# FoX and dilated attention trunk on one core: the value product in two 64-column halves, issued between the scores and the transposes of a tick

## What is computed

```
for i in range(DEPTH):                       # 2 layers
    h = rmsnorm(x, norm[i])
    x = x + (fox_attention(h) if i % 2 == 0 else dilated_attention(h))
    x = x + square(relu(rmsnorm(x, mlp_norm[i]) @ w1[i])) @ w2[i]

# one head of one group, for a block of queries
s = q @ k.T * scale + bias_or_mask
p = softmax(s)
o = p @ v                                    # the value product
```

## Time and profile before

| | us |
|---|---|
| median of 3 runs | 1651.6 |
| lowest and highest | 1650.48, 1652.94 |
| the profiled execution, its own time | 1654.75 |
| its span from first to last instruction | 1653.0 |
| PE busy | 1611.0 (97%) |
| PE weight loads busy | 1363.1 (82%) |
| DVE busy | 818.0 (49%) |
| ACT busy | 600.4 (36%) |
| POOL busy | 355.3 (21%) |
| mean granted clock of PE | 0.994 |

### The profile page before, as it was taken

How to read it: one execution, slowest core, us unless ns; L and a number is a source line. 1 busy time by engine, 2 the same in 40 slices (tenths; PEclk the granted TensorE clock), 3 DMA queues, 4 the chain that set the end, 5 groups by cost and what they waited for, 6 DMA issues and landing times.

```text
span 1653.0 us, 21763 instructions
## 1 busy us (share of the span) xinstructions
PE 1611.0 (97%) x8058; PEld 1363.1 (82%) x8066; DVE 818.0 (49%) x1468; ACT 600.4 (36%) x1068; POOL 355.3 (21%) x534
## 2 busy tenths in 40 slices
PE   7999988999999999999999999999999999999999
PEld 6777766888888888899998899998777888888887
DVE  4356566444343444444646576546565443435342
ACT  5433332342323233434434443434342432424230
POOL 3412100050000000263527364535711000000000
PEclk9999999999999999999999999999999999999999
DMA  5311110323232323332222412222223232323232
GB/s 169 90 51 39 57 34 3 100 88 104 89 105 85 114 77 104 126 90 77 66 75 77 128 53 77 64 77 64 77 79 103 78 113 87 104 89 102 89 101 78
DMA packets 77556, 139.83 MB, mean 85 GB/s; under 512 B 12192, under 2 KB 12192, under 8 KB 77216
## 3 DMA queue, kind: packets, MB, share of 16 engines
q1 hardware_dynamic: 75280, 134.51, 26.6%
q10 hardware_dynamic: 2192, 4.20, 0.7%
HBM read 132.33 MB, written 6.36 MB: 84 GB/s over the span
## 4 chain that ended last, share of the span: by engine, by line
PE 85%; DVE 5%; POOL 4%; issue 2%; ACT 2%; SPq 1%; DMA 0%; ACTq 0%; POOLq 0%; DVEq 0%
PE ps L467 74%; PE ps L553 3%; PE ps L525 3%; POOL qrs L1330 2%; PE ps L539 2%; PE ps L565 1%; POOL qss L1329 1%; DVE pT_sb L1110 1%; PE ps L498 1%; ACT w_h L784 1%; DVE qss L1021 1%; PE ps L519 1%; ACT p_sb L848 1%; ACT sq L822 1%; DVE negmax L1075 0%
## 5 line engine op out<-in xcount | busy, mean ns | idle before, releaser
L467 PE MATMUL ps<-w_h,act_h 128*128 128x512 f32 x768 | 317.3, 413 | 5.7 <-DVE w_l L995 3.4
L467 PE MATMUL ps<-w_h,act_l 128*128 128x512 f32 x768 | 306.9, 400 | 0.0
L467 PE MATMUL ps<-w_l,act_h 128*128 128x512 f32 x768 | 305.7, 398 | 0.0
L784 ACT ACTIVATE w_h<-w_raw,gain_t 128x512 fp32r<-128x512 f32 x316 | 209.8, 717 | 150.4 <-PE ps L467 102.7
L995 DVE SCALAR_TENSOR_TENSOR w_l<-w_raw,gain_t,w_h 128x512 fp32r<-128x512 f32 x316 | 226.6, 759 | 58.4 <-ACT w_h L784 58.4
L467 PE MATMUL ps<-w_h,hid_h 128*128 128x512 f32 x640 | 252.5, 395 | 0.2
L467 PE MATMUL ps<-w_l,hid_h 128*128 128x512 f32 x640 | 250.0, 391 | 0.0
L467 PE MATMUL ps<-w_h,hid_l 128*128 128x512 f32 x640 | 249.7, 390 | 0.0
L467 PEld LDWEIGHTS ps<-w_h,act_h 128*128 128x128 f32 x768 | 192.2, 250 | 24.0 <-issue 8.0
L467 PEld LDWEIGHTS ps<-w_l,act_h 128*128 128x128 f32 x768 | 192.5, 251 | 15.2
L467 PEld LDWEIGHTS ps<-w_h,act_l 128*128 128x128 f32 x768 | 193.4, 252 | 13.5
(11 more groups left out here) (150 smaller groups left out, 1935.8 us busy)
## 6 DMA issues: line engine op xcount, KB each, us to landing
w_raw<-in_mlp_w SPq DMA_DIRECT2D x128, 512.0 KB, 3.7
w_raw<-in_dil_w_in SPq DMA_DIRECT2D x72, 512.0 KB, 3.7
w_raw<-in_fox_w_in SPq DMA_DIRECT2D x22, 512.0 KB, 3.6
w_raw<-in_fox_w_out SPq DMA_DIRECT2D x8, 512.0 KB, 3.7
w_raw<-in_dil_w_out SPq DMA_DIRECT2D x8, 512.0 KB, 3.8
acc_kept<-acc SPq DMA_DIRECT2D x2, 1056.0 KB, 6.4
o_sb<-acc_kept SPq DMA_DIRECT2D x2, 1056.0 KB, 5.1
x_sb<-in_x SPq DMA_DIRECT2D x4, 512.0 KB, 8.4
```

Source lines behind the costliest of these rows:

```text
L467: return mm(ps_out, lhs[i], rhs[j], start=(k == 0 and term == 0), stop=(k == KT - 1 and term == 2))
L784: last = fn(w_h[:, u % WR, j, :], raw(u)[:, j, :], ACT.Copy, scale=gain_t[:, norm, k:k + 1])
```

## The change

Two edits in the PE program, none elsewhere.

1. Each value matmul of a 128x128 stationary block becomes two, with the block's columns 0 to 63 and 64 to 127 as the stationary operand. The first writes partitions 0 to 63 of the output bank, the second 64 to 127. The moving operand is the same for both. 400 matmuls become 800. In the built program the halves carry the array tile (128 rows, 64 columns) at column 0 and at column 64, where the whole block had (128, 128).
2. Within a tick, `values` (of three ticks ago) is called ahead of `turn_probs` (of two ticks ago), so it stands directly behind the scores where the tick has any.

```diff
--- before.py
+++ after.py
@@ -550,8 +550,10 @@
                 c = 0
                 for q, k0, nk in SCORE_BANKS[SETS[s][0]][i]:
                     for k in range(nk):
-                        last = mm(o_ps[:, q, 0:VC], pT_sb[:, a % 2, c * P:(c + 1) * P], v_sb[s % 2][:, k0 + k, h // 2, head_cols(h)],
-                                  start=(k == 0), stop=(k == nk - 1))
+                        for side in range(2):
+                            rows = slice(side * P // 2, (side + 1) * P // 2)
+                            last = mm(o_ps[rows, q, 0:VC], pT_sb[:, a % 2, c * P + rows.start:c * P + rows.stop],
+                                      v_sb[s % 2][:, k0 + k, h // 2, head_cols(h)], start=(k == 0), stop=(k == nk - 1))
                         c += 1
                 last.then_inc(pv_done, 1)
 
@@ -574,10 +576,10 @@
                             pe.wait_ge(qt_done, QK_SET * (attend + 1))
                         if a < nt and a % 2 == 0:
                             scores(attend, t0 + a)
+                        if 3 <= a <= nt + 2:
+                            values(attend, t0 + a - 3)
                         if 2 <= a <= nt + 1:
                             turn_probs(attend, t0 + a - 2)
-                        if 3 <= a <= nt + 2:
-                            values(attend, t0 + a - 3)
                     for s, b in turns_of_tick(proj, attend, a):
                         turn_qk(s, b)
                     if proj is None:
```

## The result

The changed kernel is slower: 1680.68 us median of 4 runs (1671.05 to 1686.98), before 1652.27 (1650.48 to 1660.79), ratio 1.0137 with a 95% interval of 1.0101 to 1.0172. Forecast were 1653.5 us and a range up to 1668. The changed kernel's runs lie much further apart than those of before, and their order is that of the granted clock: 1671 us at a mean of 0.994, 1677 at 0.991, 1685 at 0.982, 1687 at 0.980. The execution profiled is this last one, 32 us of span above the one before, so it shows more of the loss than the median does (28 us). A straight line through the four times against their mean clocks gives 1666 us at a clock of 1.000; one through the 19 executions of the kernel before that were measured beside the first experiments gives 1648. By this estimate, good to a few us with only four points, about 18 us of the loss are there at full clock, and the rest is the clock.

What follows compares the result with a forecast made beforehand. PE bounds steps with filler, the scores-DVE-exponentials round the other two. Halves -27.5, shape changes +16.8, order +1.8 and +6, steps without filler +4.5 sum to +1.6 us; against a 1651.6 us median, forecast 1653.5, range 1640 to 1668.

Steps and rivals of the forecast that it cites:

- What bounds the kernel: PE time in steps with filler (projection matmuls); in (None,1) and (None,7), the round from scores over DVE to exponentials.
- Part 1, the halves: Value blocks in steps with filler: halves pair up, 0.059 us a pair instead of 0.111, a gain of 27.5 us.
- the rival in which they take turns: Value blocks: the two halves run one after another, so no pairing gain; about 1686 us, chance 0.15.
- Part 2, the change of shape: 72 value blocks in steps with filler: PE loses time switching between whole array and halves, 16.8 us (11 to about 24).
- Part 3, the order with filler: Steps with filler: dearer way from transposes to filler, 1.8 us, and lost cover of waits for DVE's output, 6 us.
- the 3 to 6 named as a sign: PE's idle time at the value line until DVE's output would grow by about 3 to 6 us if right.
- Part 4, the steps without filler: Steps (None,1) and (None,7): later transposes delay DVE, and the clock may lose a little; 4.5 us (0 to 10).
- The claim that the late copy matters in 8 pairs of ticks: Steps (None,1) and (None,7): DVE's copy ends 0.45 us later in 4 + 4 pairs of ticks, 3.6 us.
- part 3b: Steps with filler: transposes no longer run inside the values' wait for DVE's output, at 11 blocks; 6 us (3 to 9).
- a little more: Steps (None,1) and (None,7): with PE idle for longer, the granted clock may cost slightly more, inside the 4.5 us.
- the waits grow: Step (1,0): 15 more value blocks wait 0.5 us each for DVE's output, slower by 4 to 15 us, 1661; chance 0.22.

Runs made afterwards that it cites:

- the first experiments: The follow-up runs starting with the order alone (1709.78 us) and the halves alone (1647.11 us), measured beside the kernel before.
- run 2: Changed kernel with the values back behind the transposes, so the halves alone against the kernel before: 1647.11 us, ratio 0.9958.
- run 6: Kernel before, with 72 added idle-time matmuls in steps (None,1) and (None,7) to keep PE busy: 1654.50 us, ratio 1.0001.
- run 3: Changed kernel with values ahead of the transposes only in steps with filler, old order in (None,1) and (None,7): 1651.37 us, ratio 0.9987.
- runs 4 and 9: Changed kernel with a third probability buffer in steps (None,1) and (None,7), 1661.53 us; the same plus 72 idle-time matmuls there, 1661.22 us.

## Why the prediction was wrong

- **What bounds the kernel**, PE where there is filler and the round over DVE where there isn't: right, and it is where the result was decided.
- **Part 1, the halves**: right. 0.62 us for a block of 16 recorded matmuls against a forecast of 0.616; the rival in which they take turns (0.15) fell, though the measured 1681 us is near its 1686. The rule named beside it, of the Trainium skill, "TensorE: Matmul & The Clock Gate", Part 3, that weight loads overlap running matmuls only where the row group differs, isn't what these rows show: both halves share all rows, and their pairs still start within 0.46 us.
- **Part 2, the change of shape**: right. 0.32 into a value block (0.33), 0.34 out of it into the filler in run 2 (0.34). One sum is written wrongly: from 88.06 + 0.11 to 88.37 it is 0.20; the 0.09 comes out with the second matmul's own slot of 0.11 added.
- **Part 3, the order with filler**: 6.2 us by the run of the order alone, a part of it the clock, and 3.6 to 4.3 with the halves (1041.7 and 1042.4 against 1038.1); 7.8 forecast. PE's idle time at the value line until DVE's output grew by 9.3 us in these steps (4.8 to 14.1), more than the 3 to 6 named as a sign. Parts 1 to 3 together were -2.9 by the sum, and the rest of the stretch came out at -0.5 (1042.4 against 1042.9) in the changed kernel and -1.2 in the run with the new order there only.
- **Part 4, the steps without filler**: wrong, and the step that decided. It said 4.5 us (0 to 10); it was 32.6 in the profiled execution. With every bound of parts 2 to 4 at its high end the sum is +17, some 1669 us, so no other size of its terms reaches the result. Three things failed in it.
  1. The claim that the late copy matters in 8 pairs of ticks, 0.45 each. It was worked out for even ticks alone, from the earlier trace rows. In odd ticks the value block itself waits for DVE's output and the transposes stood ahead of that wait; behind it they hold DVE's copy up by 0.79 us. That was the same loss of cover that part 3b counts where there is filler, and part 4 left it out. Near full clock the late copy and output come to 7.6 us (against run 6) to 10.5 (against run 3) instead of 3.6; the 0.45 itself is by the prediction's own times 236.1 - 235.57 = 0.53.
  2. The exponentials' wait for the transposes (`pt_full`, two buffers) was missing. Part 3b asked who waits behind the value block and named DVE and the filler, and of the exponentials only that the transposes wait for them. The other direction costs 3 to 4 us by itself, and most of the lower clock came by way of it (runs 4 and 9).
  3. The clock was "a little more". It is 20 us of the profiled execution and about 13 of the median. The row was there: a mean of 0.94 with PE busy 44.6 of 55 us says that the lower level is granted at times in this step even before the change. How much more of it the longer rounds would bring, the row doesn't say; the prediction left it some 0.9 us of the 4.5 without working it out.
- The rival *the waits grow* had a part of the mechanism, DVE's outputs that come too late, but its place was the step (1,0), and it was priced without the clock at 1661 us. Its chance was 0.22. The chances gave slower by over 0.2% 0.37 in all, by causes that aren't the one measured.

## What to carry to other kernels

When an instruction is moved ahead of another on an engine, list who waits for the one that is now later, in each stage of the kernel, buffers to be freed included; a wait that was covered in one stage can be the pace of another. Where a stage already shows a granted clock below 1, added waits there can cost more than their length (here 20 us of 32.6), and a run that keeps the engine busy tells the two apart. Try the move stage by stage: here the two parts of the change had opposite signs, and the halves alone (1647 us, ratio 0.9958) beat the kernel before and the changed one.

## What the runs showed of the hardware

- Two 64-column stationary blocks at columns 0 and 64, both of 128 rows and float32, run side by side: eight pairs of recorded matmuls in 0.46 us from first to last start. Their loads are recorded with a mean of 138 ns in run 2, against 192 for 128 columns in the kernel before:

```profile
L555 PEld LDWEIGHTS ps<-v,pT_sb 128*64 128x64 f32 x1600 | 56.8, 138 | 36.9 <-issue 23.0 <-DVE pT_sb L1112 14.0
```

- The gain of pairing is mostly given back by the changes of shape, 0.28 to 0.34 us for each block that stands alone, against an estimate of 8 x 0.052 = 0.42 gained in a block of four. In the steps with filler 4.8 us were left of it (run 2).
- The clock fell to its lower level in stretches where PE was still recorded as busy for most of the time: 70.9 of 91 us in the changed kernel, at a mean of 0.77. The recorded busy share of a step doesn't tell the level: with the third buffer it was nearly the same, 56.3 of 73 us, at a mean of 0.98 (211 to 284 us). What decides between the two stays open.
